# Routing of a mixture of experts: fewer repeated copy matmuls around the ranks, the rests of the scaled rows in quarters, the group mask in one step

## The reference, cut to what matters

```
h2 = modulate(rms_norm(x, g_norm2), sh2, sc2)
g_logits = h2 @ w_rg + b_rg                      # 4 groups
e_logits = h2 @ w_re + b_re                      # 4 x 8 experts
g_idx    = argmax(g_logits)                      # one group for each token
e_val, e_loc = top_k(e_logits of that group, 2)  # two experts inside it
e_w      = softmax(e_val) * softmax(g_logits)[g_idx]
for each expert: y = (silu(h @ w1) * (h @ w3)) @ w2, for the tokens that chose it
x = x + ga2 * (sum of the experts' y by their weights)
```

## Time and profile before

| | us |
|---|---|
| median of 3 runs (1203.63 to 1204.74) | 1204.32 |
| the profiled execution, its own time | 1205.15 |
| span of the profiled execution | 1203.3 |
| PE busy | 1149.5 (96%) |
| DVE busy | 487.0 (40%) |
| ACT busy | 409.8 (34%) |
| mean granted TensorE clock | 0.984 of full speed |

### The profile page before, as it was taken

How to read it: one execution, slowest core, us unless ns; L and a number is a source line. 1 busy time by engine, 2 the same in 40 slices (tenths; PEclk the granted TensorE clock), 3 DMA queues, 4 the chain that set the end, 5 groups by cost and what they waited for, 6 DMA issues and landing times.

```text
span 1203.3 us, 15528 instructions
## 1 busy us (share of the span) xinstructions
PE 1149.5 (96%) x5906; PEld 762.1 (63%) x5906; DVE 487.0 (40%) x967; ACT 409.8 (34%) x607; POOL 231.5 (19%) x104
## 2 busy tenths in 40 slices
PE   4899999999999999999989988899999999999998
PEld 1578767774444444544434435888877778888886
DVE  1595552752222222222212215789454653333226
ACT  3533444232111111211112105664244363534334
POOL 0362233300000000000000003400313335442522
PEclk8899999989999999999999999999999999999999
DMA  9986366679899999999999995533213464654541
GB/s 377 342 303 247 141 225 258 270 295 377 329 389 422 422 422 422 422 422 422 422 421 422 421 420 196 210 138 135 79 71 140 149 205 145 198 153 180 203 160 50
DMA packets 89193, 331.68 MB, mean 276 GB/s; under 512 B 3873, under 2 KB 26690, under 8 KB 62514
## 3 DMA queue, kind: packets, MB, share of 16 engines
q1 hardware_dynamic: 88512, 330.36, 70.5%
q0 software_dynamic: 432, 0.48, 0.2%
q10 hardware_dynamic: 194, 0.06, 0.0%
HBM read 329.84 MB, written 1.05 MB: 275 GB/s over the span
## 4 chain that ended last, share of the span: by engine, by line
PE 74%; DMA 17%; DVE 5%; ACT 1%; issue 1%; SPq 1%; POOL 0%; DVEq 0%; ACTq 0%
DMA ring<-in_w 15%; PE ps L832 14%; PE ps L833 13%; PE ps L834 13%; PE ps L1150 13%; PE ps L1192 5%; DMA ring<-in_w_ada 2%; PE ps L1122 1%; PE ps L892 1%; PE ps L1123 1%; PE ps L1303 1%; SPq L721 1%; ACT ring_r L1502 1%; PE ps L946 1%; PE ps L944 1%
## 5 line engine op out<-in xcount | busy, mean ns | idle before, releaser
L807 POOL TENSOR_TENSOR ring_r<-ring,ring_r 128x1024 fp32r<-128x1024 f32 x80 | 207.3, 2611 | 819.2 <-ACT ring_r L1502 819.2
L1150 PE MATMUL ps<-ring,arena 128*64 128x512 f32 x1008 | 225.9, 596 | 8.6 <-DMA ring<-in_w 7.5
L833 PE MATMUL ps<-ring_r,hl_r 128*128 128x512 f32 x528 | 211.5, 400 | 0.0
L832 PE MATMUL ps<-ring_r,hl_r 128*128 128x512 f32 x480 | 197.5, 411 | 12.0 <-DVE ring_r L1924 5.1
L834 PE MATMUL ps<-ring_r,hr_r 128*128 128x512 f32 x480 | 192.5, 401 | 0.0
L1502 ACT ACTIVATE ring_r<-ring 128x2048 fp32r<-128x2048 f32 x90 | 167.2, 1907 | 63.1 <-PE ps L834 44.9
L1150 PEld LDWEIGHTS ps<-ring,arena 128*64 128x64 f32 x1008 | 69.5, 137 | 148.8 <-issue 127.6
L1924 DVE TENSOR_TENSOR ring_r<-ring,ring_r 128x2048 fp32r<-128x2048 f32 x50 | 118.3, 2373 | 92.3 <-ACT ring_r L1502 92.1
L832 PEld LDWEIGHTS ps<-ring_r,hl_r 128*128 128x128 f32 x480 | 92.0, 192 | 41.0 <-issue 18.3
L833 PEld LDWEIGHTS ps<-ring_r,hl_r 128*128 128x128 f32 x528 | 101.2, 192 | 22.3
L834 PEld LDWEIGHTS ps<-ring_r,hr_r 128*128 128x128 f32 x480 | 91.9, 191 | 22.4
(11 more groups left out here) (363 smaller groups left out, 1656.8 us busy)
## 6 DMA issues: line engine op xcount, KB each, us to landing
ring<-in_w SPq DMA_DIRECT2D x91, 2048.0 KB, 21.5
ring<-in_w_in SPq DMA_DIRECT2D x21, 2048.0 KB, 8.1
ring<-in_w_ada SPq DMA_DIRECT2D x8, 2048.0 KB, 9.0
ring<-in_w_ffn_gate SPq DMA_DIRECT2D x11, 1024.0 KB, 5.2
ring<-in_w_ffn_up SPq DMA_DIRECT2D x11, 1024.0 KB, 7.7
ring<-in_w_ffn_down SPq DMA_DIRECT2D x5, 2048.0 KB, 7.7
ring<-in_w_ada SPq DMA_DIRECT2D x8, 1024.0 KB, 10.1
ring<-in_w_o SPq DMA_DIRECT2D x2, 2048.0 KB, 7.7
```

The lines of the kernel that those rows point to most:

```text
L807: nc.gpsimd.tensor_tensor(rest[:, a:b], w[:, a:b], lead[:, a:b].bitcast(F32), ALU.subtract).then_inc(sem("w_rest_b"), 1)
L832: mm(o, lhsT=a_lead, rhs=b_lead, start=start, stop=False, skip_group_check=True)
L833: mm(o, lhsT=a_lead, rhs=b_rest, start=False, stop=False, skip_group_check=True)
L1150: last = mm(H[slots_of(e), :], lhsT=xs[:, k, slots_of(e)], rhs=w, start=k == 0, stop=k == KD - 1)
```

## The change

On PE, the two repeats ahead of the ranks go, and of the two repeats behind them one stays, so that one `keep_x(..., True)` is left of four. `gather` gets a flag for the first time it is used: instead of one wait ahead of each half it waits twice inside of it, at j = 0 and j = 2.

On DVE, `first_max` can return the complement of its one-hot (`ALU.not_equal`), and the mask of the other groups is made in one step for each token tile: minus BIG times "other group", plus the logit, two unlinked instructions of 128x32 in place of one linked of 128x8 and two linked of 128x64. `x1_rests` gets a first block and a count: a call covers blocks `at` to `at + n` of a half. The first two blocks of half 0 are made where half 0 was made, the last two between `one_hot(0)` and the release of the bank of the ranks, and half 1 where it was.

```diff
             for n in range(4):
                 keep_x(n)
-            keep_x(0, True)
-            keep_x(1, True)
             o = small.claim(pe, "rank")
...
-            keep_x(2, True)
-            keep_x(3, True)
+            keep_x(0, True)
             for name in small_order[n_block1 - 4:n_block1]:
                 pe.wait_ge(*small.released[name])
 
-            def gather(n):
+            def gather(n, first=False):
 
                 for j in range(4):
+                    if first and j % 2 == 0:
+                        pe.wait_ge(sem("xp_rest"), 6 if n else j + 2)
...
                 for n in range(2):
-                    pe.wait_ge(sem("xp_rest"), 2 * n + 2)
-                    gather(n)
+                    gather(n, True)
...
-            gsel = rt[:, 1, :, 0:GROUPS]
-            first_max(g, GROUPS, r1[:, 0, :], gsel, rt[:, 2, :, 0:GROUPS], r1[:, 1, :])
+            other = rt[:, 1, :, 0:GROUPS]
+            first_max(g, GROUPS, r1[:, 0, :], other, rt[:, 2, :, 0:GROUPS], r1[:, 1, :], ALU.not_equal)
...
-            link(v.tensor_scalar(rt[:, 2, :, 0:GROUPS], gsel, BIG, -BIG, ALU.mult, ALU.add))
...
-            link(v.tensor_tensor(by_group(rt[:, 3, :, :]), by_group(e), per_group(gsel), ALU.mult))
-            link(v.tensor_tensor(by_group(rt[:, 4, :, :]), by_group(rt[:, 3, :, :]), per_group(rt[:, 2, :, 0:GROUPS]), ALU.add))
+            for t in range(TT):
+                mark(v.scalar_tensor_tensor(rt[:, 4, t, :].rearrange("p (g n) -> p g n", g=GROUPS),
+                                            other[:, t, :].unsqueeze(2).to_broadcast([P, GROUPS, PER_GROUP]), -BIG,
+                                            e[:, t, :].rearrange("p (g n) -> p g n", g=GROUPS), ALU.mult, ALU.add))
+            settle()
...
-            x1_rests(0)
+            x1_rests(0, 0, 2)
             src = small.ready(dve, "rank")
...
             one_hot(0)
+            x1_rests(0, 2, 2)
             release(v.tensor_reduce(flagf[:, 0:1], src[0:1, 64:96], AX.X, ALU.max), small, "rank")
             v.tensor_scalar(flag[:, :], flagf[:, 0:1], float(CAP), None, ALU.is_gt).then_inc(sem("flag_ready"), 1)
-            x1_rests(1)
+            x1_rests(1, 0, 4)
```

More of the change, by code:

```diff
@@ L2105, in wide_, with first_max @@
                 return a.unsqueeze(2).to_broadcast([P, TT, n])
-            def first_max(values, n, best, one_hot, tmp, least):
+            def first_max(values, n, best, one_hot, tmp, least, taken=ALU.is_equal):
                 link(v.tensor_reduce(best, values, AX.X, ALU.max))
@@ L2112, in first_max @@
                 link(v.tensor_reduce(least, tmp, AX.X, ALU.min))
-                link(v.tensor_tensor(one_hot, tmp, wide_(least, n), ALU.is_equal))
+                link(v.tensor_tensor(one_hot, tmp, wide_(least, n), taken))
             g, e = lg[:, :, 0:GROUPS], lg[:, :, GROUPS:]
-            gsel = rt[:, 1, :, 0:GROUPS]
-            first_max(g, GROUPS, r1[:, 0, :], gsel, rt[:, 2, :, 0:GROUPS], r1[:, 1, :])
+            other = rt[:, 1, :, 0:GROUPS]
+            first_max(g, GROUPS, r1[:, 0, :], other, rt[:, 2, :, 0:GROUPS], r1[:, 1, :], ALU.not_equal)
             v.tensor_tensor(rt[:, 7, :, 0:GROUPS], g, wide_(r1[:, 0, :], GROUPS), ALU.subtract).then_inc(sem("route_sub_ready"), 1)
-            link(v.tensor_scalar(rt[:, 2, :, 0:GROUPS], gsel, BIG, -BIG, ALU.mult, ALU.add))
             def by_group(a):
                 return a.rearrange("p t (g n) -> p t g n", g=GROUPS)
-            def per_group(a):
-                return a.unsqueeze(3).to_broadcast([P, TT, GROUPS, PER_GROUP])
-            link(v.tensor_tensor(by_group(rt[:, 3, :, :]), by_group(e), per_group(gsel), ALU.mult))
-            link(v.tensor_tensor(by_group(rt[:, 4, :, :]), by_group(rt[:, 3, :, :]), per_group(rt[:, 2, :, 0:GROUPS]), ALU.add))
+            for t in range(TT):
[3 more added lines that the diff above has]
+            settle()
             first_max(rt[:, 4, :, :], EXPERTS, r1[:, 2, :], rt[:, 1, :, :], rt[:, 3, :, :], r1[:, 1, :])
@@ L2134, in _, with x1_rests @@
             v.tensor_tensor(r1[:, 5, :], r1[:, 3, :], r1[:, 2, :], ALU.subtract).then_inc(sem("route_sub_ready"), 1)
-            def x1_rests(h):
+            def x1_rests(h, at, n):
                 for t in range(TT):
                     dve.wait_ge(sem("xp_ready"), 2 * h + t + 1)
-                    v.scalar_tensor_tensor(xp_r[t][:, 4 * h:4 * h + 4, :],
-                                           x[:, t, h * COL:(h + 1) * COL].rearrange("p (q j) -> p j q", j=4), rs[:, 1, t:t + 1],
-                                           xp_l[:, t, 4 * h:4 * h + 4, :].bitcast(F32), ALU.mult,
+                    blocks = slice(4 * h + at, 4 * h + at + n)
+                    v.scalar_tensor_tensor(xp_r[t][:, blocks, :],
+                                           x[:, t, h * COL:(h + 1) * COL].rearrange("p (q j) -> p j q", j=4)[:, at:at + n, :],
+                                           rs[:, 1, t:t + 1], xp_l[:, t, blocks, :].bitcast(F32), ALU.mult,
                                            ALU.subtract).then_inc(sem("xp_rest"), 1)
-            x1_rests(0)
+            x1_rests(0, 0, 2)
             src = small.ready(dve, "rank")
```

## The result

The changed kernel is slower. Over 14 executions of each, its median is 1209.38 us against 1204.28 of the kernel before; the ratio is 1.0039, 95% interval 1.0028 to 1.005, on the undisturbed executions alone. (One execution of the changed kernel took 2910 us and is left out of the ratio; it has no profile, and its cause is not known. Without it the median of the other 13 is 1209.19.) The profiled execution took 1208.86 us, its span is 1207.0: 3.7 us over the 1203.3 of before.

The account below looks back on a forecast made before the run. PE, not DVE, was taken to set when the ranks come and thus the weight stream's end. Terms: -0.66 us of gain, +3.4 for the clock's fall, -0.1, sum +2.6: 1206.9 on the median, range 1203.2 to 1208.9.

Parts of the forecast that it names:

- The two repeats ahead: PE ahead of the ranks: four matmuls go, 1.72 us, so the ranks start at 262.52 instead of 264.24.
- The mask: DVE's choice of experts: 0.37 us instead of 0.72, a gain of 0.35 hidden by the copies, worth nothing.
- The quarters: DVE's rests as 128x512 split into 128x256 at 0.53 us each; half 1's rests come only 0.66 us earlier.
- The waits: Inside the first gather: finer waits worth nil; PE idle 1.6 us ahead of it and 0.4 between halves.
- The carry: From PE's shift at 271 us to the weight stream and the end: passed on in full, taken as 1.
- The clock: PE behind the ranks: granted clock falls at some point of the gather, losing 3.4 us, less some 0.1.
- This one begins in the gather: 6.8: Length of the low-clock stretch, begun in the gather: 6.8 us, half of it lost; likeliest case, chance 0.38.
- The second rival: Low stretch of another length: three times 3.4 us from ahead of gather(0), 1208.5 (0.14); a single 3.4, 1205.3 (0.08).
- its 0.66 of gain: Sum at an unchanged clock: the rests of half 1, gather(1) and w1 come 0.66 us earlier.
- the base: Profiled kernel before, 1205.15 us with slow copies; the same +2.6 us was put on the median of 1204.32.
- The rival in which the clock stays: Granted clock 1.00 from 264 to 276: -0.66 us on the profiled execution, 1203.7 on the median; chance 0.34.

Follow-up runs that it names:

- Three repeats behind: Changed kernel with three wide repeats behind the ranks instead of one, none ahead: median 1204.45 us, ratio 0.9972 to 1.0004 against the kernel before.
- the copies alone: Kernel before with only the repeats changed, none ahead of the ranks and one behind, DVE as before: median 1209.16 us, ratio 0.9997 to 1.0033.
- two repeats ahead: Changed kernel with the two repeats ahead of the ranks put back, one still behind: median 1209.07 us, ratio 1.0004 to 1.0034.
- the narrow fill: Changed kernel plus eight narrow copies of 32 columns behind its one wide repeat: median 1210.43 us, ratio 1.0017 to 1.0045; output not the reference's.
- the release first: Changed kernel with the release of the ranks' bank and the flag ahead of the second pair of quarters: median 1207.73 us, ratio 1.0 to 1.0024.
- a wide repeat between the halves: Changed kernel with the ranks' bank released before the second quarters, plus one wide repeat ahead of gather(1): median 1205.80 us, ratio 0.9984 to 1.0013.
- none and one repeat ahead: Kernel before with one-step mask, two repeats behind, whole rests; none ahead of the ranks: median 1202.96 us, one ahead: 1206.14 us.
- the mask alone: Kernel before with only the mask made in one step, all four repeats kept: median 1204.63 us, ratio 0.9966 to 1.0003.

## Why the prediction was wrong

The direction and the mechanism of the forecast were right, the size was not: 1206.9, up to 1208.9, and 1209.38 measured. It gave 0.60 to a fall of any length, and 0.14 to the case that came nearest. By its own steps:

- *The two repeats ahead* were to bring the ranks 1.72 us forward, with PE last. In the profile after they came when DVE had chosen, after 2.12 us of idle time, since the copies met the full clock. The prediction named this case, but did its sum for the slow one. Three repeats behind, with slow copies, showed the step as priced.
- *The mask*: 0.37 us expected, 0.32 measured (258.46 to 258.78).
- *The quarters*: 0.53 each expected, 0.57 to 0.59 measured; the release is 2.30 us behind the start of the slots in place of 2.21, the rests of half 1 2.57 in place of 2.49.
- *The waits*: 1.6 us idle ahead of the gather expected, 1.73 measured, ended by the release. The finer waits did nothing. The 0.4 us between the halves went, because the slow gather took longer than the rests.
- *The carry*: the end of w1 came 4.2 us later than before (282.30 against 278.10), the end of the span 3.7.
- *The clock* falls, as forecast: at 263.9, ahead of the gather instead of inside it. **The step that failed is where the low stretch begins and how long it lasts**, "This one begins in the gather: 6.8". It was 13.7 us, and 13.7 again in the profiles of the copies alone and of the changed kernel run again; that is longer than the longest case of the range, three times 3.4. Where the fall did begin in the gather, with two repeats ahead, it lasted the 6.8 us of the forecast. Some 2.3 us of the 13.7 lie ahead of the gather, where PE mostly waits; in the 11.4 left, gather and w1 lose 5.1 us, as the split above shows, in place of 3.4.

I took the length from stretches that narrow work only began, 1.1 us of it at 255. Here 7.0 us of gather follow at the low clock, which the low clock itself has nearly doubled, and it came back only 4.4 us into w1. With the narrow fill the stretch was 17.1, with the release first 10.2, and with a wide repeat between the halves 6.8. I also left out a stretch of 10.2 us in the trace of before itself (19.5 to 29.7, with PE idle up to 23.8). And of the 1.1 us in which PE was busy at 716.5 to 719.2, the four transposes are only 0.71; the rest is the start of wide matmuls at 718.81.

The second rival came closest: a fall ahead of `gather(0)`, both gathers doubled, 5.1 us lost, 1208.5. The loss is the measured one, 3.11 + 1.97; only its length, three times 3.4, was too short. With the measured losses in the forecast's sum, and its 0.66 of gain, it would have been +4.4: 1208.7.

The second fault is the base. The price was set against a profile in which the kernel before had itself lost time to slow copies. The prediction saw that the fall costs more against executions without that, but gave it no number: an estimated 22.7 us against 24.4. How often the kernel before meets the low clock there isn't on record. If its median holds both kinds, the loss lies between 3.5 and 5.2; the middles of the two ratios are +4.7 and +3.3, the second just below that.

The rival in which the clock stays is refuted for the changed kernel, by two profiles and by the granted clock of its executions. The Trainium skill's account ("TensorE: Matmul & The Clock Gate", the section on HAM oscillation), falls by long waits in which PE does nothing, doesn't cover this case: the release-first kernel, with 2.13 us idle ahead of the ranks and 0.72 ahead of the gather, fell too, and with two repeats ahead the clock fell inside a gather that ran without a gap. Whether transposes count for less than other narrow matmuls no run here separates.

What stays open: which share of the falls the idle time ahead of the ranks has (the copies alone, with 0.47 us idle behind, fell as well), and the 3 us between none and one repeat ahead. The profiles alone don't rule out another reading, either. Of the seven in which the copies ran at the full clock, six show a fall behind the copies and only the mask alone doesn't; of the six in which the copies met the low clock, only two ahead shows one. That the repeats behind the ranks matter, and not only how the copies met the clock, rests on the medians and the mean granted clocks of all executions.

## What to carry to other kernels

Work that repeats a result can be what holds TensorE's clock: before taking it out, look what is left around it, idle time and matmuls of few columns alike, up to the next wide ones. Price a fall by all narrow work that will run at the low clock, which takes nearly twice as long and didn't end it here, plus the first of the wide work: in the six profiles in which the clock was still low when w1 began, it came back 2.3 to 4.8 us into it. And put a release ahead of work that is needed only later: two quarters ahead of it cost 1.16 us here where PE was waiting.

## What the hardware showed that I had not expected

- A low stretch can outlast 11 us of unbroken matmuls: in the changed kernel 6.9 us of gather with PE busy 6.88, then 4.4 us of w1, all at 0.50; with the narrow fill 16.9 us.
- The clock fell in the middle of a gather that ran without a gap (270.6, with two repeats ahead), 2.4 us behind the idle time that came before it.
- Kernels with the same PE instructions up to the copies met the clock differently there: in seven of the 13 profiles the copies ran at the full clock, in three the low one lasted 3.4 us and in three 6.8.
